# Eight expert slots, a ninth chunk ahead, and a loop body of two expert pairs in a hybrid decoder step

## The reference, cut to what matters

```
top_v, top_i = lax.top_k(x @ w_router + b_router, 4)       # 264 tokens, 32 experts
gates = softmax(top_v)
for each expert e, for the tokens routed to it:
    gate, up = split(x @ w_gate_up[e] + b_gate_up[e])       # 1024 x 2048
    gate = minimum(gate, 7); up = clip(up, -7, 7)
    y += gates * ((up + 1) * gate * sigmoid(1.702 * gate)) @ w_down[e] + b_down[e]   # 1024 x 1024
y = rmsnorm(h + y)
```

## Time and profile before

| | |
|---|---|
| median of the runs | 1453.68 us |
| the profiled execution | 1453.18 us |
| its span in the trace | 1451.2 us |
| PE busy | 1409.3 us, 97% |
| DVE busy, ACT busy | 449.0 us, 219.1 us |
| moved by DMA | 494.61 MB, mean 341 GB/s |
| chain that ended last | PE 78%, DMA 19% |

### The profile page before, as it was taken

One profiled execution on the slowest core, in us unless ns is written; L12 is line 12 of the kernel. 1 busy time (PEld: TensorE's weight loads), 2 busy tenths in 40 slices (PEclk: granted clock), 3 DMA queues, 4 the chain that ended last, 5 costly groups with the idle time before them and its releaser, 6 DMA issues.

```text
span 1451.2 us, 15871 instructions
## 1 busy us (share of the span) xinstructions
PE 1409.3 (97%) x6277; PEld 691.6 (48%) x6277; DVE 449.0 (31%) x909; ACT 219.1 (15%) x390; POOL 28.1 (2%) x48
## 2 busy tenths in 40 slices
PE   7999999999999899999999999999999999999997
PEld 5888887678757533333323333333333333333332
DVE  4734344861551331212112222132122221221213
ACT  2220022052122300101001000010010100100102
POOL 0000002200000000000000000000000000000000
PEclk9999999999999999999999999999999999999999
DMA  6653435975288189999999999999999999999993
GB/s 225 209 165 129 146 115 184 372 274 193 104 316 356 62 363 428 427 428 430 428 427 430 429 428 429 429 427 429 428 429 428 429 429 427 429 427 429 429 428 139
DMA packets 69758, 494.61 MB, mean 341 GB/s; under 512 B 8427, under 2 KB 9859, under 8 KB 45133
## 3 DMA queue, kind: packets, MB, share of 16 engines
q1 hardware_dynamic: 65164, 478.60, 80.1%
q0 software_dynamic: 4368, 15.53, 3.0%
q10 hardware_dynamic: 196, 0.07, 0.0%
HBM read 486.12 MB, written 8.22 MB: 341 GB/s over the span
## 4 chain that ended last, share of the span: by engine, by line
PE 78%; DMA 19%; ACT 1%; issue 1%; SPq 1%; DVE 0%; DVEq 0%; ACTq 0%
PE bank L1370 73%; DMA ring<-in_w_gate_up 19%; PE bank L1381 5%; SPq L464 1%; PE bank L1807 0%; DMA flat<-in_x_sample 0%; ACT projT L552 0%; ACT projT L561 0%; DVE projT L1311 0%; DVE projT L1289 0%; DVE projT L1352 0%; ACT projT L825 0%; DVE xnT L858 0%; SPq L401 0%; ACT hT L561 0%
## 5 line engine op out<-in xcount | busy, mean ns | idle before, releaser
L1370 PE MATMUL bank<-ring,projT 128*64 128x512 f32 (+1 forms) x2080 | 460.9, 595 | 20.0 <-DMA ring<-in_w_gate_up 19.5
L1370 PEld LDWEIGHTS bank<-ring,projT 128*64 128x64 f32 (+1 forms) x2080 | 149.2, 136 | 311.4 <-issue 308.8
L1370 PE MATMUL bank<-xnT,ring 128*128 128x264 f32 x1152 | 266.7, 390 | 1.1 <-DVE xnT L858 1.1
L1370 PEld LDWEIGHTS bank<-xnT,ring 128*128 128x128 f32 x1152 | 218.0, 191 | 43.0 <-issue 5.8
L1370 PE MATMUL bank<-flat,projT 128*64 128x512 f32 (+2 forms) x536 | 231.4, 591 | 0.0
L1370 PE MATMUL bank<-conv,projT 128*64 128x512 f32 (+1 forms) x528 | 229.6, 594 | 0.0
L1370 PE MATMUL bank<-projT 128*128 128x512 f32 (+4 forms) x536 | 220.3, 550 | 1.6 <-ACT projT L552 1.3
L1370 PEld LDWEIGHTS bank<-projT 128*128 128x128 f32 (+3 forms) x536 | 73.6, 169 | 146.2 <-issue 97.2
L1370 PEld LDWEIGHTS bank<-flat,projT 128*64 128x64 f32 (+2 forms) x536 | 71.2, 137 | 137.7 <-issue 137.1
L1331 DVE TENSOR_SCALAR projT<-bank 128x512 f32<-128x512 f32 x32 | 20.6, 686 | 343.5 <-PE bank L1370 343.5
L812 ACT ACTIVATE projT<-projT 128x512 f32<-128x512 f32 x32 | 19.6, 630 | 550.0 <-DVE projT L1331 550.0
(11 more groups left out here) (252 smaller groups left out, 680.3 us busy)
## 6 DMA issues: line engine op xcount, KB each, us to landing
ring<-in_w_gate_up SPq DMA_DIRECT2D x96, 2048.0 KB, 16.2
ring<-in_w_down SPq DMA_DIRECT2D x32, 2048.0 KB, 13.0
ring<-in_w_in SPq DMA_DIRECT2D x16, 2048.0 KB, 13.2
flat<-in_w_gate_up SPq DMA_DIRECT2D x16, 2048.0 KB, 14.0
conv<-in_w_gate_up SPq DMA_DIRECT2D x16, 2048.0 KB, 18.4
flat<-in_w_down SPq DMA_DIRECT2D x16, 2048.0 KB, 15.8
conv<-in_w_down SPq DMA_DIRECT2D x16, 2048.0 KB, 20.2
ring<-in_w_xk SPq DMA_DIRECT2D x2, 2048.0 KB, 9.2
```

The lines of the kernel that those rows point to most:

```text
L1370: last[0] = pe.matmul(out, lhsT, rhs, start=start, stop=stop)
```

## The change

The order of the early jobs in PLAN changes: `dt` and `dtt` come later. The banks of `mrow` 1 and of `srow` change. In SBUF, `projT` and `mnT` become one tensor `wide`, `hT` and `xnT` one tensor `tokT`, and `xgt` and `gfin` get memory of their own (`bdn` lies in `gfin`). The six slots get three more:

```
+        mslot += [x.rearrange("p (k n) -> p k n", k=8) for x in (
+            first_acts, tokT[:].rearrange("p s a b -> p (s a b)")[:, 0:4096], wide[:, GB * T:GB * T + 4096])]
+        RING = [0, 1, 2, 3, 4, 5, 7, 8]
+        FIRST_SLOT = [0, 1, 2, 3, 4, 5, 6, 7, 8, 0, 1, 2]
+        AHEAD = 9
```

`first_acts` (slot 6) is the memory of gate, up, sig and actT, which the first pair writes only after its part 3. The loads of experts on SP:

```
             for j, name, k in ((2, "so", 1), (4, "so", 1), (5, "so", 3), (0, "so", 3), (1, "xo", 3), (3, "xo", 7)):
                 filled(sp, name, k)
-                if j == 5:
-                    sp.dma_start(gfin, a["norm_final"].partition_broadcast(P)).then_inc(S["gfin_in"], 16)
                 sp.dma_start(chunk_view(j, j), moe_chunk(0, j)).then_inc(moe_full[j], 16)
+            filled(sp, "rs")
+            sp.dma_start(chunk_view(8, 8), moe_chunk(0, 8)).then_inc(moe_full[8], 16)
+            filled(sp, "xtok", 5)
+            sp.dma_start(chunk_view(7, 7), moe_chunk(0, 7)).then_inc(moe_full[7], 16)
+            sp.wait_ge(S["mrows_out"], 32)
+            sp.wait_ge(S["srows_out"], 32)
+            sp.dma_start(chunk_view(6, 6), moe_chunk(0, 6)).then_inc(moe_full[6], 16)
             sp.wait_ge(S["passes_ready"], 1)
             n = sp.value_load(npass[0:1, 0:1], min_val=0, max_val=MAXP - 1)
-            with sp.Fori(0, n * PAIRS + (PAIRS - 1)) as it:
-                for j in range(6, 18):
-                    if j % 2 == 0:
-                        sp.wait_ge(S["stage_done"], it * 6 + (j // 2 - 2))
-                    pair = it % PAIRS if j < 12 else (it + 1) % PAIRS
-                    sp.dma_start(chunk_view(j % 6, j % 12), moe_chunk(pair, j % 12)).then_inc(moe_full[j % 6], 16)
+            def refill(g, pair):
+                i, j = RING[(g - AHEAD) % 8], g % 12
+                sp.dma_start(chunk_view(i, j), moe_chunk(pair, j)).then_inc(moe_full[i], 16)
+            for g, done_stages in zip(range(AHEAD, AHEAD + 8), (1, 1, 2, 2, 3, 3, 4, 5)):
+                sp.wait_ge(S["stage_done"], done_stages)
+                refill(g, g // 12)
+            with sp.Fori(0, n * (PAIRS // 2) + (PAIRS // 2 - 1)) as it:
+                for g in range(17, 41):
+                    sp.wait_ge(S["stage_done"], it * 12 + ((g - 8) // 2 + 1))
+                    refill(g, (it * 2 + g // 12) % PAIRS)
+            for g in range(12 * PAIRS - 7, 12 * PAIRS):
+                sp.wait_ge(S["stage_done"], n * (6 * PAIRS) + ((g - 8) // 2 + 1))
+                refill(g, PAIRS - 1)
+            sp.wait_ge(S["ytok_ready"], 2)
+            sp.dma_start(gfin[:], a["norm_final"].partition_broadcast(P)).then_inc(S["gfin_in"], 16)
```

The waits for `mrows_out` and `srows_out` leave DVE (L1297, L1298). On PE, DVE and ACT the body becomes a function `experts`, called once for the first pair, twice in a loop of 7 rounds, once for the last pair with `final=True`; the last pair has no gather, no transposes of gathered rows, no selection and no one-hot for a next pair:

```
+            experts(first_pair, 0)
+            with pe.Fori(0, n * (PAIRS // 2) + (PAIRS // 2 - 1)) as it:
+                for which in range(2):
+                    experts(next_pair(it, which), 1 + which, it)
+            experts(last_pair(n), PAIRS - 1, final=True)
+            scatter(beyond(n))
```

At the start, the sample's tile is loaded first, PE transposes the sample and prompt tile 0 and after that prompt tile 1, the first weight chunk comes in two halves of 256 columns, `wdt`, `dtb` and `alog` are issued before weight 3 instead of weight 1, ACT takes the roots before the copies of the transposes, and PE issues two unread matmuls at once:

```
+            pe.wait_ge(S["ones_set"], 1)
+            for _ in range(2):
+                pe.matmul(bank[7][:, :], ones[:], ones[:, 0:1].to_broadcast([P, 512]), start=True, stop=True)
             pe.wait_ge(S["consts_set"], 2)
-            for t in range(3):
+            for t in (2, 0):
                 pe.wait_ge(x_in[t], 16)
             for k in range(KB):
                 b = free_bank(pe, "xT", k)
-                for t, (c, n) in enumerate(TILES):
+                for t in (2, 0):
+                    c, n = TILES[t]
                     turn(b[:, c:c + n], xtokin[0:n, t, k * P:k * P + P])
+            pe.wait_ge(x_in[1], 16)
+            for k in range(KB):
+                turn(bank[BANK[JOB["xT", k]]][:, P:2 * P], xtokin[:, 1, k * P:k * P + P])
                 close("xT", k)
...
-            xb(0, 1)
-            pe.wait_ge(wdt_in, 16)
...
+            xb(0, 1, 2, 3)
             pe.wait_ge(mem_in, 32)
             mem_turns(0, 1)
             xb(4)
             mem_turns(2, 3)
             xb(5)
+            step_width()
...
-         ("rt", 3, D_, (2, 6, 7)), ("rs", 1, A_, (1,)), ("xtok", 3, A_, (3, 4, 5)), ("mrow", 3, A_, (0, 6, 7)),
-         ("srow", 2, A_, (1, 0)), ("rank", 1, D_, (2,))]
+         ("rt", 3, D_, (2, 6, 7)), ("rs", 1, A_, (1,)), ("xtok", 3, A_, (3, 4, 5)), ("mrow", 3, A_, (1, 6, 7)),
+         ("srow", 2, A_, (0, 3)), ("rank", 1, D_, (2,))]
...
             emptied(pe, "xtok", 5)
-            stay_warm(4)
+            stay_warm(2)
```

More of the change, by code:

```diff
@@ L571, in root @@
                     .then_inc(sem_, 1)
-            for k in range(8):
-                move("xT", k, hT[:, k, :], T)
             s.wait_ge(S["x_summed"], 3)
@@ L577, in _ @@
             root(rtok, slice(2, 3), TS, S["x_root"])
+            for k in range(8):
+                move("xT", k, hT[:, k, :], T)
             move("par0", 0, par[:, 0, :], P)
@@ L1312, in accumulate, with experts @@
                     .then_inc(S["scat_read"], 1)
-            with v.Fori(0, n * PAIRS + PAIRS) as it:
-                st.n, st.off = n0, it * 5
-                pair = it % PAIRS
-                v.wait_ge(S["xy_full"], it * 2 + 2)
-                select(it * 2 + 2)
-                v.wait_ge(S["gt_full"], it + 1)
-                st(ranked(selG, it * 2))
+            def experts(at, pair, after, final=False):
+                if not final:
+                    v.wait_ge(S["xy_full"], at(2, 2))
+                    select(at(2, 2))
+                v.wait_ge(S["gt_full"], at(1, 1))
+                st(ranked(selG, at(2, 0)))
                 v.tensor_tensor(out=slots_of(selG), in0=slots_of(selG), op=ALU.mult,
@@ L1405, in project @@
                 for j in ks:
-                    w = chunk_in(pe, weights + str(j // 4))
+                    if name == "xb" and j < 2:
+                        pe.wait_ge(first_half, 16)
+                        w = mslot[0]
+                    else:
+                        w = chunk_in(pe, weights + str(j // 4))
                     b = free_bank(pe, name, j)
@@ L1806, in stay_warm @@
                 for _ in range(times):
-                    pe.matmul(bank[3][:, 0:256], ident[:], bgu[:, 0:256], start=True, stop=True)
+                    pe.matmul(bank[5][:, 0:256], ident[:], bgu[:, 0:256], start=True, stop=True)
             pe.wait_ge(S["bias_in"], 128)
@@ L1904, in down @@
                 def down(part):
-                    landed(part)
-                    w = [chunk_view((2 * part + e) % 6, 2 * part + e) for e in range(2)]
+                    w = landed(part)
                     for m in range(4):
```

264 lines of the change are left out of this document (152 added, 112 removed).

## The result

The changed kernel takes 1441.77 us (median of 4 runs, 1440.32 to 1443.06) where the kernel before takes 1455.44 on the same chip: a ratio of 0.9915, 95% interval 0.990 to 0.9929. A second series gave 1440.09 to 1453.39, 0.9911 [0.9897, 0.9924]. That is 13 to 14 us faster.

What follows compares the result with a forecast made beforehand. The prediction took the expert loop to be bound by the rate of its weight loads, not by PE. Experts 10.3, last pair 0, start 5.0 and passage 4.8 summed to 20.1 us saved: 1433.6 us, range 1427 to 1442.

Steps and rivals of the forecast that it cites:

- Experts: Expert loop: nine chunks loaded ahead instead of six save 14.7 us, less a 4.4 us hole: minus 10.3 us.
- Start: From kernel begin through the first projections: earlier transposes and a faster clock, less 0.9 for late loads: minus 5.0 us.
- projection at 13.0: At the start: with fast transposes, ACT's copies end at 11.9 and the first projection begins at 13.0, 3.8 us won.
- so I take the fast end: At the start: unread matmuls were taken to bring full clock, giving 5.9 us won rather than 2.6.
- Passage: Between attention and experts: no bank wait and two unread matmuls instead of four bring rank earlier: minus 4.8 us.
- Last pair: Last pair of experts, without gather and its transposes: taken as 0, bounds 1.7 us won and 1.6 lost.
- Reloaded code: Rival, expert loop: the doubled body must fetch instructions at each jump back, up to 1495 us; chance 0.04.
- Loads as they are, start and passage give little: Rival: late mem_prompt, dt or clock leave 10.3 + 3 + 0 to 2 us, 1438 to 1440; chance 0.15.
- PE becomes the bound: Rival, expert loop: faster loads leave PE's 913.4 us, gaining 22.6 instead of 10.3: 1421 us; chance 0.07.
- slower rate: Rival, expert loads: more queues lower the rate, 3% of 895 us costing 27, about 1460; chance 0.02.
- Chunk 6 late: Rival, before the experts: stores hold up chunk 6 so it gives no lead, 4.9 us less, 1438; chance 0.05.
- The hole or the clock costs less: Rival, experts and start: 13 to 14.7 us instead of 10.3, and 5.9: 1428 to 1430; chance 0.10.

Runs made afterwards that it cites:

- b1_eight: Changed kernel with eight weight slots from the start and no ninth chunk, waits for stored rows back on DVE; 1442.26 us, ratio 0.9922.
- a4: Changed kernel without the two unread matmuls ahead of the transposes at the start; 1439.83 us (kernel before: 1453.23).
- a7: As a1_whole, with three more unread matmuls of 512 columns behind rbc, where PE waits for weights; 1437.44 us (kernel before: 1453.73).
- a1_whole: Changed kernel with the first weight chunk loaded in one piece instead of two halves; 1440.98 us (kernel before: 1452.93).
- g_after: The changed kernel unaltered, run again in a second series; 1440.09 us, ratio 0.9911 to the kernel before.
- d1_again: Second run of changed kernel plus whole first chunk, earlier memory root, later state copies, unread matmuls at start, first and last pair; 1434.79 us, ratio 0.9875.
- d2: Changed kernel with the old start, three unread matmuls behind rbc, later state copies, unread matmuls at first and last pair; 1439.23 us, ratio 0.9897.
- a2_twoq: Changed kernel with the first weight chunk split by rows, half issued on SP's queue and half on ACT's; 1439.84 us.

## Why the prediction was right and wrong

**Experts: right, but for the clock.** The step "186 x 4.893" to "183 x 4.893", less a hole, gave 10.3, that is 895.97 us from the first bias to the last wait. In the ten profiles with nine chunks and the full clock at the first bias it is 896.0 to 896.9, a gain of 9.3 to 10.3; in the other four, bias 1.85 to 2.09, it is 897.9 to 899.0. The hole of 4.4 us measured 3.5 (by the prediction's own terms, 550.1 + 2.5 is 552.6, which makes it 4.1). What failed is "with these durations": the durations of stage 1 were those of a fast clock, and no price stood for a slow one ahead of the first refill, though all that the change wins here hangs on when stage 1 ends. It cost 1.7 us directly (1.91 + 7.97 against 1.14 + 7.09) and 2.0 by the last wait. The first long wait in pair 9 and the eight waits came as forecast; the loads end at about 1413, forecast 1404, since the whole loop lies later than forecast.

**Start: wrong, and most of the miss: + 1.46 for - 5.0.** Three steps failed. First, "projection at 13.0": the prediction followed PE and ACT, and took the first weights to be there. It named x and `mem_prompt` as loads and never priced the first chunk, nor the parameters. The trace of before has the chunk's landing, in the timeline of SP and in the list of the DMA issues of the first 3 us (count, KB, us from issue to landing):

```profile
2.13 0.41 SPq L450 DMA_DIRECT2D ring<-in_w_in  x1
...
ring<-in_w_in SPq DMA_DIRECT2D x1, 2048.0 KB, 14.6
```

That is 16.7 us, just ahead of the projection at 16.76: the old start stood at that bound already, though the row names DVE as what it waited for, and with these loads no earlier projection was to be had. After the change it lands at 17.0. The parameters land at 13.49, and by b1_eight, where 2.61 us lie between their transpose and the projection, they alone would have held it until about 16.1 (an estimate). Instead of 3.8 us won, 0.25 were lost, 4.05 us of the miss. Second, "so I take the fast end": the transposes did begin at 5 and started fast, but the clock fell at 9, under them, and the 64 records behind the waits ran slow, so that the 2.1 us to be won became 0.42 lost, 2.5 us of the miss. Removing the unread matmuls ahead of the transposes changed nothing (a4), adding three in the last gap gave 2.35 us (a7). The Trainium skill, TensorE: Matmul & The Clock Gate, HAM oscillation, describes a wait for a load after which the work starts at the slow clock each time. The trace of a1_whole agrees, where the clock falls within a wait of 5.24 us and 16.86 us follow for what takes 14.51; in the changed kernel's the slow work follows on 3.62 and 1.67 us of waits too, but the clock had fallen before them. I had cited the general rule for the gain, and should have asked what PE does in the last us before the projection. Third, the late root: the "none to 3" for late loads was the wrong item; `mem_prompt` was in time, and what was late was a root behind two changes of ACT's function table, 0.53 us of waiting (0.63 in all; 0.9 had been taken off).

**Passage: right.** 5.2 for 4.8 (4.1 in g_after, where the transposes are slow), and `rank` is bound by its mask as predicted. The stores that share the engines with chunks 7 and 8 took 5.7 to 7.8 us instead of 2.0 to 2.8, within the ten allowed; chunk 6 was issued at 497.17, not at about 490, but early enough: it landed 7.6 us later, ahead of the first refill at 506.58 and of its use in part 3.

**Last pair: right.** The forecast was 0 between - 1.7 and + 1.6; it is - 0.2 here, and up to + 1.0 in the other profiles without an edit to it (44.2 to 45.4 us behind the last wait). Activations come as worked out and the clock falls as feared; d1_again, at full clock, ends 43.0 us after the last wait, 1.2 less.

**Rivals.** *Reloaded code*: false. The seven branches of the new loop take 76 to 249 ns (median 208), and of the packets of instructions, 27 on one queue and 11 on another (21 and 9 before), none lies between 700 and 1300 us. The Trainium skill, Runtime: NRT & Kernel Launch, Instruction fetch mechanics, has room for 2048 instructions on PE, and the trace agrees: a body of more than 1000 records of PE is not fetched again. *Loads as they are, start and passage give little*, 1438 to 1440, was the nearest, for one of its reasons: the clock, not `mem_prompt`. It had 0.15. *PE becomes the bound* and *slower rate*: false, 429 GB/s and a share of 1.01. *Chunk 6 late*: false. *The hole or the clock costs less*: the hole did, the clock didn't. No rival had the ninth chunk. It proved nearly worthless (0.2 to 1.1 us), as the sum could have said, since 4.9 us of lead bought a hole of 3.5 to 4.4.

The largest error of judgement is that the start's two unsure terms, the weights and the clock, were both taken at their good end.

## What to carry to other kernels

Before a stage of the engine is pulled forward, find the load it will meet next, and read when it landed in the old kernel (its issue plus its time to landing): a load that nobody waited for can still be a bound, 0.03 us behind the one that shows. Ask the same of every small load that the stage needs. In a kernel bound by a stream of loads, what counts is when the stream starts and how long it stands, and the stage that frees the first slot is on that path at whatever clock it gets. Unread matmuls helped here only in the last gap ahead of the work that they were to speed up, and only where the engine was idle for longer than they took (a7 against a4 and d2).

## What the runs showed of the hardware

- The landing of the first weights hardly moves, whatever the kernel does around it: 16.7 before the change, 17.0 (half of the chunk, rows of 1 KB), 17.1 (whole, rows of 2 KB), 17.0 (two queues), 16.5 (old order), 15.9 to 16.6 without GpSimd's copies. At 8 to 16 us the share of the DMA engines is 0.39 to 0.73 in all profiles but one, so they aren't full (a2_twoq, with two queues, reaches 1.00 and 383 GB/s from 12 to 16 us). What the first chunk waits for is not settled.
- The granted clock falls at a different place from one execution to the next of the same program: at 481 (transposes 3.91 us) in one, at 496 (bias 1.91 us) in another, and each fall costs 1.3 to 2 us. Neither place has an idle time of PE above 0.5 us just ahead of it. At the start it fell at 9 us, with PE busy. In the last pair the same two gaps (0.30 and 1.40 us) were followed by slow work in two executions and by fast work in two. What sets it off wasn't isolated.
- The column of the granted clock can read 1.00 over matmuls that run slow: 64 records took 16.72 us in a4_nostart with the column at 1.00 in every window from 8 to 24 us, and 14.51 us in a7_startwarm. Durations are the safer witness.
- A load of another function table on ACT took 1.28 us, and the next operation began right behind it (51.12, 52.42).
